# Fourier mixing by halves: a shorter DFT, head mixing folded into the weights, and the convolution's norm computed inside the attention

## The chip, the cores and the metric

The kernel runs on one core of a Trainium2 chip, in one launch, in float32 throughout. The metric is device time in microseconds of one execution; the median of several runs is compared. TensorE multiplies matrices (results land in PSUM banks of 512 float32 columns), ScalarE applies functions, VectorE does elementwise work and reductions, GpSimd small copies, and DMA queues issued from SyncE and ScalarE bring the weights from HBM.

## The reference, cut to what matters

Two networks run one after the other on 256 tokens of width 1024. The first has two layers; each projects the input (x, and in layer 0 also a context of 256 tokens, "two streams"), and mixes tokens in three branches: windowed attention, a convolution and a Fourier branch. The branches are gated by silu of projected gates and go through `w_out`. The parts that the change touches are these:

```
def conformer_conv(a, b_glu, conv_w, conv_b, ln_g, ln_b):
    u = a * jax.nn.sigmoid(b_glu)
    y = depthwise_conv(u, conv_w) + conv_b          # 31 taps, 256 channels
    return jax.nn.silu(layer_norm(y, ln_g, ln_b))

def fourier_mix(u, w_four, b_four):
    bn, n = u.shape[0], u.shape[1]
    uh = u.reshape(bn, n, FOUR_HEADS, FOUR_HEAD_DIM).astype(jnp.float32)
    f = jnp.fft.fftn(uh, axes=(1, 3), norm='ortho').real
    f = f.reshape(bn, n, FOUR_W).astype(u.dtype)
    return f @ w_four + b_four
```

The transform runs over 256 tokens and over the 64 channels of each of 4 heads. Its real part is the cosine transform over tokens mixed by the cosine matrix over channels, minus the sine transform over tokens mixed by the sine matrix over channels. The second network (a projection of 49 tiles, three attentions, gates, 16 experts) is not touched.

## The kernel before, in words

Every engine runs its own instruction list; the lists meet at semaphores. TensorE's order is written out by hand in `_(pe)`. Two PSUM banks `lin` and two `aux` are used in turn: `lin_bank` (L385) waits until the bank of two turns ago has been taken by ScalarE, `aux_bank` (L394) the same for VectorE. Weights stream from HBM in units of 1 MB into a ring of 6 slots (L861 to L874); SyncE loads a slot when TensorE has freed it. The last stage, the 16 experts, also loads units aside, into buffers that are free by then.

Layer 0 begins with the ada projection (L588, `ada_step`), then the norm, then the input tiles, `TILES1`, each a `product` of 8 accumulated matmuls of 512 columns (L607 to L610): the convolution's CB and CA tiles, the keys KK, the four query tiles QQ, a Fourier gate, and last the token-major tiles (values and Fourier input, L515) and the second Fourier gate (L525). In layer 1 most tiles have 256 columns. ScalarE copies each tile out of PSUM (L1057); for KK and QQ it also writes four quarters to RT (`half_turned`, L945), from which VectorE makes the rotary embedding (L1280). VectorE runs the convolution's 62 taps between the ropes (L1345 to L1366).

Between the last tile and the attention stands the stretch that the change rewrites (L611 to L645). TensorE computes the mean of the convolution over channels (L618), the DFT over tokens (L626; for each stream and each of 2 channel tiles a bank of 512 columns, 256 cosine and 256 sine), the variance (L631), the head mixing by the block matrices bc and bs (L637, L638), and the product with w_four (L643). VectorE subtracts the mean (L1370), squares (L1374), copies the DFT out to CS (L1378), takes the reciprocal of the norm (L1380), multiplies it in (L1382), copies the mixed result to FF (L1385) and adds b_four (L1388). ScalarE takes the square root (L1063) and applies the convolution's silu (L1067).

Attention (L538, L974, L1289) runs in pairs of items, 16 pairs in layer 0 and 8 in layer 1. For pair p TensorE computes scores (L551), transposes the probabilities of pair p-1 (L564) and multiplies pair p-2 by the values (L577). VectorE adds the mask and takes the maximum (L1313, L1316), ScalarE the exponential (L997), VectorE scales (L1297, L1301), ScalarE copies the transposes to PT (L987). Between these TensorE does "fills", matmuls of gate tiles (L456) and ada steps (L486). After attention ScalarE applies silu to the 8 gate tiles in the order `MIX_ORDER` (L1072), VectorE multiplies them in (L1397), and TensorE runs the output projection in the same order (L433 into aux).

Of the kernel before, what the change touches and what calls it, by code (L numbers as in the profile page):

```python
# [20 lines left out]
ALU = mybir.AluOpType  # L21
# [12 lines left out]
PAD = CONV_K // 2  # L34
N_EXP, EPG, TOPK = 16, 4, 64
# [30 lines left out]
MIX_ORDER = (4, 5, 6, 7, 0, 1, 2, 3)  # L66
# [38 lines left out]
for _name, _w in [("cos", 256), ("sin", 256), ("dft0", 512), ("dft1", 512), ("bc", 128), ("bs", 128),  # L105
                  ("band0", 512), ("band1", 512)]:
    C1[_name] = (_n, _n + _w)
    _n += _w
# [10 lines left out]
def constants():  # L119
# [24 lines left out]
    cs = np.concatenate([np.cos(ang), np.sin(ang)], 1)  # L144
# [20 lines left out]
def build(nc, w_stream, x_in, mem_in, cols_in, wfour_in, wsmall_in, c0_in, c1_in, c2_in, gf_in, rows, out):  # L165
    ctx = ExitStack()
    with ctx:
# [28 lines left out]
        wfour = sb("wfour", [P, DEPTH, 2, 256])  # L196
        wsmall = sb("wsmall", [P, KT, 24])
# [4 lines left out]
        warm = sb("warm", [P, 1])  # L202
# [15 lines left out]
        CS = G1[:, 0:2048].rearrange("p (f s n) -> p f s n", f=2, s=2)  # L218
        FF = G1[:, 2048:3072].rearrange("p (f s n) -> p f s n", f=2, s=2)
# [29 lines left out]
        for name, w in (("logits", 20), ("of_group", 16), ("place", 16), ("d", 5), ("e", 5), ("group", 4), ("sub", 4),  # L249
# [30 lines left out]
        roped, conv_done, conv_sq, conv_norm, conv_act = (  # L280
            sem(n) for n in ("roped", "conv_done", "conv_sq", "conv_norm", "conv_act"))
# [99 lines left out]
        def _(pe):  # L381
# [214 lines left out]
            for layer in range(DEPTH):  # L596
                L = f"l{layer}"
                ns = 2 if layer == 0 else 1
                for t in TILES1:
# [3 lines left out]
                    if t == GF + 1:  # L603
                        token_tiles((L, "tok"), [(H[:, s], tt, 384 if s < ns else P) for s in range(2) for tt in range(TT)],
                                    lambda: (lin_bank((L, GF + 1)), n, rhs))
                        continue
                    bank = lin_bank((L, t))  # L607
# [3 lines left out]
                if layer == 0:  # L611
                    pe.wait_ge(consts_in, 3 * 16)

                n = ns * SEQ
                pe.wait_ge(conv_done, layer + 1)
# [1159 lines left out]
```

## Time and profile before

| | |
|---|---|
| median of 3 runs | 1175.64 us (1171.31 to 1178.19) |
| profiled execution | 1173.04 us, span 1169.9 us |
| TensorE busy | 1074.7 us |
| VectorE busy | 406.0 us |
| ScalarE busy | 331.6 us |
| HBM traffic | 232.91 MB read |
| chain that ended last | PE 78%, DMA 12%, DVE 4%, ACT 3% |

In the profile PE is TensorE's matmuls and PEld its weight loads, DVE is VectorE, ACT ScalarE, SP SyncE. A float32 matmul stands in it as two records. The chain that ended last is followed back from the last instruction, at each step to what released it; a shorter step on it makes the program shorter as long as nothing else is then later. The granted clock is the share of 2.4 GHz that the chip allowed TensorE.

### The profile page before, as it was taken

Reading aid. Unit: us, or ns where it says so; the run is one execution under the profiler, and the core shown is the slowest. Engines: PE = TensorE matmul, PEld = TensorE weight load, DVE = VectorE, ACT = ScalarE, POOL = GpSimd, SP = SyncE. Lnnn points to the kernel's source line nnn. Section 1 sums busy time; section 2 is a strip of 40 time slices with the busy share of each in tenths; the row PEclk is TensorE's granted clock in tenths of the full one; section 3 lists DMA queues with packets and bytes.
Section 4 is the critical chain, followed back from the end, with each engine's and each line's share of the span. In section 5 each row is a group of like instructions: output and inputs, shape, how many; then the busy total and the mean of one; then the engine's idle time right before and its main releaser. Section 6 shows DMA issues by size and latency. Waiting matters only on the chain.

```text
span 1169.9 us, 13568 instructions
## 1 busy us (share of the span) xinstructions
PE 1074.7 (92%) x4952; PEld 676.1 (58%) x4952; DVE 406.0 (35%) x1182; ACT 331.6 (28%) x772; POOL 13.5 (1%) x60
## 2 busy tenths in 40 slices
PE   3899989999979998999999989879999998998885
PEld 0344434444457677768888456668888743443332
DVE  3269154432258444613932014641112400000004
ACT  2222133332043345234553024640011311111102
POOL 0000000000000000000000000000000000000010
PEclk9899999999989999999999999999999899999998
DMA  9897016452133222443433432036444589999995
GB/s 371 362 340 273 36 36 272 164 212 72 72 131 122 72 73 75 182 146 142 144 144 144 154 117 90 1 162 270 144 148 160 214 350 420 424 424 423 424 423 217
DMA packets 32903, 238.38 MB, mean 204 GB/s; under 512 B 3696, under 2 KB 3952, under 8 KB 6768
## 3 DMA queue, kind: packets, MB, share of 16 engines
q1 hardware_dynamic: 28768, 204.48, 44.9%
q10 hardware_dynamic: 3504, 31.06, 7.0%
q0 software_dynamic: 576, 2.10, 0.4%
q8 instruction: 35, 0.57, 0.2%
q14 instruction: 20, 0.16, 0.0%
HBM read 232.91 MB, written 19.40 MB: 216 GB/s over the span
## 4 chain that ended last, share of the span: by engine, by line
PE 78%; DMA 12%; DVE 4%; ACT 3%; issue 1%; SPq 1%; ACTq 0%; DVEq 0%
PE lin L433 28%; DMA ring<-w_stream 10%; PE aux L433 10%; PE lin L515 8%; PE sc L456 6%; PE lin L812 6%; PE aux L717 3%; PE aux L812 3%; DMA PT<-w_stream 3%; PE sc L551 2%; PE lin L564 2%; PE aux L577 2%; PE sc L771 2%; PE sc L486 1%; ACT S L997 1%
## 5 line engine op out<-in xcount | busy, mean ns | idle before, releaser
L433 PE MATMUL lin<-H,ring 128*128 128x256 f32 (+1 forms) x1360 | 341.9, 413 | 5.6 <-ACT H L1038 3.8
L433 PEld LDWEIGHTS lin<-H,ring 128*128 128x128 f32 x1360 | 261.5, 193 | 85.2 <-issue 51.3
L812 PE MATMUL lin<-ring,PR 128*64 128x512 f32 x400 | 94.5, 623 | 15.6 <-DMA ring<-w_stream 14.6
L515 PE MATMUL lin<-ring,H 128*128 128x512 f32 (+2 forms) x256 | 90.1, 513 | 0.0
L433 PE MATMUL aux<-Y,ring 128*128 128x512 f32 (+1 forms) x256 | 84.9, 493 | 3.1 <-DVE Y L1397 3.1
L812 PEld LDWEIGHTS lin<-ring,PR 128*64 128x64 f32 x400 | 32.2, 142 | 76.1 <-issue 76.1
L433 PEld LDWEIGHTS aux<-Y,ring 128*128 128x128 f32 x256 | 49.1, 192 | 38.2 <-issue 32.3
L515 PEld LDWEIGHTS lin<-ring,H 128*128 128x128 f32 x256 | 46.3, 190 | 42.7 <-issue 30.1
L456 PE MATMUL sc<-H,ring 128*128 128x512 f32 (+1 forms) x192 | 70.8, 503 | 0.0
L987 ACT ACTIVATE PT<-lin 128x512 f32<-128x512 f32 (+3 forms) x96 | 43.7, 467 | 93.3 <-PE lin L564 93.2
L1354 DVE SCALAR_TENSOR_TENSOR UN<-UN,cols 128x512 f32<-128x512 f32 (+1 forms) x120 | 64.5, 610 | 0.0
L953 ACT ACTIVATE RT<-lin 32x256 f32<-32x256 f32 x168 | 63.0, 375 | 2.6 <-DVE PR L1287 0.6
L997 ACT ACTIVATE S<-S,ST 128x513 f32<-128x513 f32 (+5 forms) x88 | 54.7, 621 | 10.6 <-DVE ST L1316 10.4
L564 PE MATMUL lin<-c,S 128*128 128x128 f32 x272 | 41.1, 285 | 13.7 <-DVE S L1301 10.1
L486 PE MATMUL sc<-ring,SC 128*32 128x512 f32 x192 | 28.5, 719 | 25.9 <-DMA ring<-w_stream 25.9
L564 PEld LDWEIGHTS lin<-c,S 128*128 128x128 f32 x272 | 31.5, 144 | 32.4 <-DVE S L1301 15.7
L456 PEld LDWEIGHTS sc<-H,ring 128*128 128x128 f32 x192 | 33.7, 189 | 27.4 <-issue 20.1
L1611 DVE TENSOR_TENSOR PR<-lin,PR 128x512 f32<-128x512 f32 x8 | 5.5, 691 | 122.7 <-PE lin L812 122.7
L717 PE MATMUL aux<-Y,ring 128*128 128x256 f32 x192 | 44.1, 390 | 3.0 <-DVE H L1478 2.5
L551 PE MATMUL sc<-PR 64*128 64x256 f32 (+3 forms) x240 | 43.3, 444 | 2.8 <-DVE ST L1313 2.1
L1297 DVE RECIPROCAL ST<-ST 128x1 f32<-128x1 f32 x88 | 14.4, 164 | 85.7 <-ACT S L997 85.0
L1284 DVE TENSOR_TENSOR RT<-RT,cb 128x256 f32<-128x256 f32 x42 | 17.8, 424 | 74.9 <-ACT RT L953 74.6
(236 smaller groups left out, 1068.8 us busy)
## 6 DMA issues: line engine op xcount, KB each, us to landing
ring<-w_stream SPq DMA_DIRECT2D x153, 1024.0 KB, 6.8
Y<-w_stream SPq DMA_DIRECT2D x14, 1024.0 KB, 15.6
UN<-w_stream SPq DMA_DIRECT2D x12, 1024.0 KB, 18.6
S<-w_stream SPq DMA_DIRECT2D x6, 1024.0 KB, 19.2
PT<-w_stream SPq DMA_DIRECT2D x6, 1024.0 KB, 20.9
rows<-PR ACTq DMA_DIRECT2D x7, 512.0 KB, 7.9
X<-x_in SPq DMA_DIRECT2D x2, 1024.0 KB, 8.4
UN<-w_stream ACTq DMA_DIRECT2D x2, 1024.0 KB, 6.4
```

The costliest lines, as they stand in the source:

```text
L433: m = mm(dst, w[:, k, :], rhs(k), start=n == 0, stop=n == KT - 1)
L456: m = mm(bank[:, 0:ns * SEQ], filling["w"][:, k, :], H[:, 0:ns, k, :], start=k == 0, stop=k == KT - 1)
L486: m = mm(bank[32 * j:32 * j + 32, :], SC[:, k0 + k, :], w[j // 2][:, 2 * k + j % 2, :], start=k0 + k == 0, stop=k0 + k == KT - 1)
L515: m = mm(bank[:, 0:width], src[:, k, tt * P:(tt + 1) * P], w[k // 4][:, k % 4, 0:width], start=k == 0, stop=k == KT - 1)
L551: m = mm(sc[:, x, a:b], it["qs"][n], it["ks"][n], start=True, stop=True, skip_group_check=True)
L564: m = tr(bank[:, j % 4 * P:(j % 4 + 1) * P], S[:, g % 4, 1 + j * P:1 + (j + 1) * P], t0("ident"))
L717: m = mm(bank[:, 0:SEQ], w[:, 4 * i + k, :], Y[:, 4 * b + k, :], start=k == 0, stop=k == 3)
L812: m = mm(bank[c, :], left[:, 4 * half + k, c], w[x][:, k, :], start=half + k == 0, stop=last)
L953: ins = fn(RT[32 * q:32 * q + 32, n % 2, :], bank[32 * r:32 * r + 32, 0:SEQ], ACT.Copy)
L987: fn(PT[:, g % 4, a:b], take()[:, 0:b - a], ACT.Copy).then_inc(lin_taken, 1)
L997: fn(e, e, ACT.Exp, bias=ST[:, g % 4, 1:2], scale=it["scale"], accum_out=ST[:, g % 4, 2:3]).then_inc(probs_ready, 1)
L1354: ins = v.scalar_tensor_tensor(out=CV[:, t, 0:ns, :], in0=u, scalar=w, in1=CV[:, t, 0:ns, :], op0=ALU.mult, op1=ALU.add)
```

## The change

The DFT matrices keep 256 of their 512 columns: the cosines of frequencies 0 to 128 and the sines of frequencies 1 to 127. The cosine half of the spectrum is even in the frequency and the sine half odd, so the other frequencies follow by adding and subtracting. The head mixing matrices bc and bs are multiplied into w_four once per layer, on TensorE, between the KK tile and the first QQ tile of layer 0; the results stay in WF. After the DFT, which now comes ahead of the mean and goes to the `lin` banks, ScalarE copies it to CS; the product with WF makes an even part (129 columns a stream) and an odd part (127 columns a stream) in one bank; VectorE writes even + b_four to frequencies 0 to 128, then even minus odd in reversed order to 129 to 255, then adds odd to 1 to 127. The mixing products, FF and its copies are gone. VectorE's reciprocal and norm of the convolution move into the attention, after the masks of pair 2. ScalarE's two silus of the convolution move behind the attention, ahead of gate 4; the gates' order becomes 6, 7, 4, 5, 0, 1, 2, 3. A load of the exponential's table is asked for ahead of attention. Each warm-up activation gets a column of its own.

```
-MIX_ORDER = (4, 5, 6, 7, 0, 1, 2, 3)
+MIX_ORDER = (6, 7, 4, 5, 0, 1, 2, 3)
...
-    cs = np.concatenate([np.cos(ang), np.sin(ang)], 1)
+    cs = np.concatenate([np.cos(ang)[:, :NYQ + 1], np.sin(ang)[:, 1:NYQ]], 1)
...
+        WF = sb("WF", [P, DEPTH, 2, 2, 256])
...
# TensorE
+                    if layer == 0 and t == QQ:
+                        pe.wait_ge(consts_in, 3 * 16)
+                        for l in range(DEPTH):
+                            for c, name in enumerate(("bc", "bs")):
+                                mm(lin_bank(("four", l, c))[:, :], t1(name), wfour[:, l, :, :], start=True, stop=True).then_inc(lin_ready, 1)
...
-                if layer == 0:
-                    pe.wait_ge(consts_in, 3 * 16)
...
+                pe.wait_ge(lin_taken, turn[L, "tok", 3] + 1)
+                for s in range(ns):
+                    bank = lin_bank((L, "dft", s))
+                    for f in range(2):
+                        for t in range(TT):
+                            m = mm(bank[:, f * 256:(f + 1) * 256], FT[:, s * TT + t, f * P:(f + 1) * P], t1(f"dft{t}"), start=t == 0, stop=t == 1)
+                    m.then_inc(lin_ready, 1)
                 pe.wait_ge(conv_done, layer + 1)
                 bank = aux_bank((L, "mean"))
...
-                pe.wait_ge(lin_taken, turn[L, "tok", 3] + 1)
-                for s in range(ns):
+                pe.wait_ge(lin_taken, turn[L, "dft", ns - 1] + 1)
+                for t in range(2):
+                    bank, c = aux_bank((L, "four", t)), slice(t * P, (t + 1) * P)
+                    even, odd = slice(0, ns * (NYQ + 1)), slice(ns * (NYQ + 1), ns * SEQ)
                     for f in range(2):
-                        bank = aux_bank((L, "dft", s, f))
-                        for t in range(TT):
-                            m = mm(bank[:, :], FT[:, s * TT + t, f * P:(f + 1) * P], t1(f"dft{t}"), start=t == 0, stop=t == 1)
-                        m.then_inc(aux_ready, 1)
+                        mm(bank[:, even], WF[:, layer, 0, f, c], CS[:, 0:ns, f, 0:NYQ + 1], start=f == 0, stop=f == 1)
+                    for f in range(2):
+                        m = mm(bank[:, odd], WF[:, layer, 1, f, c], CS[:, 0:ns, f, NYQ + 1:], start=f == 0, stop=f == 1)
+                    m.then_inc(aux_ready, 1)
...
-                for f in range(2):
-                    pe.wait_ge(aux_taken, turn[L, "dft", ns - 1, f] + 1)
-                    bank = aux_bank((L, "mix", f))
-                    mm(bank[:, 0:n], t1("bc"), CS[:, f, 0:ns, 0:256], start=True, stop=False)
-                    mm(bank[:, 0:n], t1("bs"), CS[:, f, 0:ns, 256:512], start=False, stop=True).then_inc(aux_ready, 1)
-                pe.wait_ge(aux_taken, turn[L, "mix", 1] + 1)
-                for t in range(2):
-                    bank = aux_bank((L, "four", t))
-                    for f in range(2):
-                        m = mm(bank[:, 0:n], wfour[:, layer, f, t * P:(t + 1) * P], FF[:, f, 0:ns, :], start=f == 0, stop=f == 1)
-                    m.then_inc(aux_ready, 1)
...
# ScalarE
+                    if layer == 0 and t == QQ:
+                        for l in range(DEPTH):
+                            for c in range(2):
+                                fn(WF[:, l, c, :, :].rearrange("p f n -> p (f n)"), take()[:, :], ACT.Copy).then_inc(lin_taken, 1)
...
+                for s in range(ns):
+                    fn(CS[:, s, :, :].rearrange("p f n -> p (f n)"), take()[:, :], ACT.Copy).then_inc(lin_taken, 1)
                 warm_up(ACT.Sqrt)
                 fn(RS[:, 0:n], take()[:, 0:n], ACT.Sqrt, bias=col("eps")).then_inc(lin_taken, 1)
-                act.wait_ge(conv_norm, layer + 1)
-                for t in range(2):
-                    v_ = CV[:, t, 0:ns, :]
-                    fn(v_, v_, ACT.Silu, bias=col(f"ln_b{layer}", t), scale=col(f"ln_g{layer}", t)).then_inc(conv_act, 1)
+                warm_up(ACT.Exp)
                 attention(L, lambda i: fill(layer, i))
                 act.wait_ge(fill_taken, 1 + len(FILLS[0]) + layer * len(FILLS[1]))
                 for k in MIX_ORDER:
+                    if k == 4:
+                        act.wait_ge(conv_norm, layer + 1)
+                        for t in range(2):
+                            v_ = CV[:, t, 0:ns, :]
+                            fn(v_, v_, ACT.Silu, bias=col(f"ln_b{layer}", t), scale=col(f"ln_g{layer}", t)).then_inc(conv_act, 1)
...
# VectorE
-                for s in range(ns):
-                    for f in range(2):
-                        v.tensor_copy(CS[:, f, s, :], take((L, "dft", s, f))[:, :]).then_inc(aux_taken, 1)
-                dve.wait_ge(lin_taken, turn[L, "var"] + 1)
-                after(step(v.reciprocal(RI[:, 0:n], RS[:, 0:n])))
                 for t in range(2):
-                    ins = v.tensor_tensor(CV[:, t, 0:ns, :], CV[:, t, 0:ns, :], RI[:, 0:n].rearrange("p (s n) -> p s n", s=ns), ALU.mult)
-                ins.then_inc(conv_norm, 1)
-                for f in range(2):
-                    v.tensor_copy(FF[:, f, 0:ns, :], take((L, "mix", f))[:, 0:n].rearrange("p (s n) -> p s n", s=ns)).then_inc(aux_taken, 1)
-                for t in range(2):
-                    bank = take((L, "four", t))
-                    v.tensor_scalar(YB[:, 6 + t, 0:ns, :], ...
+                    bank, y, b = take((L, "four", t)), YB[:, 6 + t, 0:ns, :], col(f"b_four{layer}", t)
...
+                    v.tensor_scalar(y[:, :, 0:NYQ + 1], even, b, None, ALU.add).then_inc(four_even, 1)
+                    dve.wait_ge(four_even, 2 * layer + t + 1)
+                    v.tensor_tensor(y[:, :, SEQ - 1:NYQ:-1], y[:, :, 1:NYQ], odd, ALU.subtract).then_inc(four_odd, 1)
+                    dve.wait_ge(four_odd, 2 * layer + t + 1)
+                    v.tensor_tensor(y[:, :, 1:NYQ], y[:, :, 1:NYQ], odd, ALU.add).then_inc(aux_taken, 1)
+
+                def conv_normed():
+                    dve.wait_ge(lin_taken, turn[L, "var"] + 1)
+                    after(step(v.reciprocal(RI[:, 0:n], RS[:, 0:n])))
+                    for t in range(2):
+                        ins = v.tensor_tensor(CV[:, t, 0:ns, :], CV[:, t, 0:ns, :], RI[:, 0:n].rearrange("p (s n) -> p s n", s=ns), ALU.mult)
+                    ins.then_inc(conv_norm, 1)
+
+                def between(p):
+                    if p == 2:
+                        conv_normed()
+                    if layer == 0 and 2 * p - 1 in ADA_TURNS:
+                        modulation(ADA_TURNS[2 * p - 1])
+
+                attention(L, between)
```

## Rows read from the trace of the kernel before

**Rows 1.** The page: busy time by engine, TensorE's.

```profile
PE 1074.7 (92%) x4952; PEld 676.1 (58%) x4952; DVE 406.0 (35%) x1182; ACT 331.6 (28%) x772; POOL 13.5 (1%) x60
```

**Rows 2.** Chain of waits, layer 0 ahead of attention: start us, us, what.

```profile
135.16 1.72 PE aux L618 x4
...
146.36 3.37 DVE RI L1380
...
157.69 1.06 PE sc L551 x4
```

**Rows 3.** Chain of waits, layer 1 ahead of attention.

```profile
384.84 3.46 PE lin L525 x16
...
397.26 1.99 PE aux L643 x8
399.26 1.06 PE sc L551 x4
```

**Rows 4.** Timeline ahead of attention: start us, us, engine, operation, [idle before <-releaser].

```profile
136.92 1.28 DVE L1370 TENSOR_TENSOR UN<-UN,aux 128x512 f32<-128x512 f32 x2 [20.53 <-PE aux L618]
...
152.29 5.40 PE L643 MATMUL aux<-PR,wfour 128*128 128x512 f32 x8 [3.26 <-DVE PR L1385]
...
155.18 0.75 DVE L1388 TENSOR_SCALAR Y<-aux,cols 128x512 f32<-128x512 f32 x1 [2.94 <-PE aux L643]
...
399.30 0.48 DVE L1388 TENSOR_SCALAR Y<-aux,cols 128x256 f32<-128x256 f32 x1 [0.38 <-PE aux L643]
```

**Rows 5.** ScalarE on the K tile (timeline); landing of w_four (DMA issues).

```profile
73.36 0.60 ACT L1057 ACTIVATE PR<-lin 128x512 f32<-128x512 f32 x1 [6.27 <-PE lin L433]
73.97 1.54 ACT L953 ACTIVATE RT<-lin 32x256 f32<-32x256 f32 x4
...
wfour<-wfour_in ACTq DMA_DIRECT2D x1, 512.0 KB, 14.5
```

**Rows 6.** Windows of 20 us: PE, PEld, DVE, ACT, POOL busy, PEclk, DMA share, GB/s.

```profile
80.00:100.00 20.00, 20.00 (x48) 8.93 (x47) 19.90 (x36) 6.30 (x15) 0.00 (x0) 1.00 1.04 365
...
140.00:160.00 20.00, 16.74 (x36) 6.72 (x36) 10.73 (x15) 5.01 (x6) 0.00 (x0) 0.91 0.00 1
...
260.00:280.00 20.00, 17.63 (x54) 8.05 (x53) 7.23 (x16) 8.81 (x15) 0.18 (x1) 0.91 0.15 53
...
320.00:340.00 20.00, 13.40 (x41) 8.80 (x40) 11.27 (x24) 11.34 (x21) 0.00 (x0) 0.74 0.28 100
...
380.00:400.00 20.00, 17.92 (x88) 13.30 (x87) 9.65 (x20) 7.11 (x12) 0.00 (x0) 1.00 0.15 53
```

**Rows 7.** Chain of waits, transposes of one item in layer 0's attention.

```profile
170.92 0.87 PE lin L564 x8
```

**Rows 8.** Timeline of layer 0's third pair: mask's last step, scaling, transposes.

```profile
170.90 0.15 DVE L1316 TENSOR_SCALAR ST<-ST 128x1 f32<-128x1 f32 x1
...
173.99 0.87 DVE L1301 TENSOR_SCALAR S<-S,ST 128x512 f32<-128x512 f32 x2
...
177.54 1.04 PE L564 MATMUL lin<-c,S 128*128 128x128 f32 x8
```

**Rows 9.** Timeline: the convolution's silus, then gates after attention in both layers.

```profile
151.07 1.52 ACT L1067 ACTIVATE UN<-UN,cols 128x512 f32<-128x512 f32 x2 [3.45 <-DVE UN L1382]
...
262.16 1.28 ACT L1072 ACT_TABLE_LOAD   x1
263.46 4.27 ACT L1072 ACTIVATE PR<-PR 128x512 f32<-128x512 f32 x8
...
265.01 7.51 PE L433 MATMUL aux<-Y,ring 128*128 128x512 f32 x13 [2.15 <-DVE Y L1397]
...
448.85 2.56 ACT L1072 ACTIVATE PR<-PR 128x256 f32<-128x256 f32 x8
```

**Rows 10.** Who the weight queue waited for; a window of the expert tail.

```profile
SPq L863 <- PE lin L433: 344.1, 43, 21.8
...
1020.00:1040.00 20.00, 20.00 (x112) 9.25 (x110) 2.03 (x6) 2.88 (x5) 0.00 (x0) 1.00 1.02 424
```

More of the change, by code:

```diff
@@ L34 @@
 PAD = CONV_K // 2
+NYQ = SEQ // 2
 N_EXP, EPG, TOPK = 16, 4, 64
@@ L104 @@
 _n = 0
-for _name, _w in [("cos", 256), ("sin", 256), ("dft0", 512), ("dft1", 512), ("bc", 128), ("bs", 128),
+for _name, _w in [("cos", 256), ("sin", 256), ("dft0", 256), ("dft1", 256), ("bc", 128), ("bs", 128),
                   ("band0", 512), ("band1", 512)]:
@@ L201, in build @@
         RO = sb("RO", [P, 192])
-        warm = sb("warm", [P, 1])
+        warm = sb("warm", [P, 16])
         CM = sb("CM", [P, TT, N_EXP])
@@ L217, in build @@
         G1 = P1[:, GA:GF, :, :].rearrange("p t s n -> p (t s n)")
-        CS = G1[:, 0:2048].rearrange("p (f s n) -> p f s n", f=2, s=2)
-        FF = G1[:, 2048:3072].rearrange("p (f s n) -> p f s n", f=2, s=2)
+        CS = G1[:, 0:1024].rearrange("p (s f n) -> p s f n", f=2, s=2)
         BVT = UN[:, 0:3072].rearrange("p (t n) -> p t n", t=TT)
@@ L279, in build @@
         dve_step = sem("dve_step")
-        roped, conv_done, conv_sq, conv_norm, conv_act = (
-            sem(n) for n in ("roped", "conv_done", "conv_sq", "conv_norm", "conv_act"))
+        roped, conv_done, conv_sq, conv_norm, conv_act, four_even, four_odd = (
+            sem(n) for n in ("roped", "conv_done", "conv_sq", "conv_norm", "conv_act", "four_even", "four_odd"))
         idx_mask, merged, gains_ready = sem("idx_mask"), sem("merged"), sem("gains_ready")
@@ L934, in _ @@
             fn = nc.scalar.activation
-            at = {"lin": 0, "sq": 0}
+            at = {"lin": 0, "sq": 0, "warm": 0}
             def take():
@@ L956, in warm_up @@
             def warm_up(f):
-                fn(warm[:, :], col("eps"), f)
+                n = at["warm"]
+                at["warm"] += 1
+                fn(warm[:, n:n + 1], col("eps"), f)
             def squares(name, src, ns, ready, between={}):
@@ L1383, in _ @@
-                ins.then_inc(conv_norm, 1)
-                for f in range(2):
-                    v.tensor_copy(FF[:, f, 0:ns, :], take((L, "mix", f))[:, 0:n].rearrange("p (s n) -> p s n", s=ns)).then_inc(aux_taken, 1)
-                for t in range(2):
-                    bank = take((L, "four", t))
-                    v.tensor_scalar(YB[:, 6 + t, 0:ns, :], bank[:, 0:n].rearrange("p (s n) -> p s n", s=ns),
-                                    col(f"b_four{layer}", t), None, ALU.add).then_inc(aux_taken, 1)
@@ L1390, in _ @@
-                attention(L, lambda p: modulation(ADA_TURNS[2 * p - 1]) if layer == 0 and 2 * p - 1 in ADA_TURNS else None)
+                for t in range(2):
+                    bank, y, b = take((L, "four", t)), YB[:, 6 + t, 0:ns, :], col(f"b_four{layer}", t)
+                    even = bank[:, 0:ns * (NYQ + 1)].rearrange("p (s n) -> p s n", s=ns)
+                    odd = bank[:, ns * (NYQ + 1):n].rearrange("p (s n) -> p s n", s=ns)
+                    v.tensor_scalar(y[:, :, 0:NYQ + 1], even, b, None, ALU.add).then_inc(four_even, 1)
[3 more added lines that the diff above has]
+                    v.tensor_tensor(y[:, :, 1:NYQ], y[:, :, 1:NYQ], odd, ALU.add).then_inc(aux_taken, 1)
```

## The prediction, made before the changed kernel was run

> **What bounds the kernel now.** I read the page first: TensorE is busy for 92% of the span [rows 1]. That only names the engine; what this change is worth depends on which wait ends last in the two places that it touches, the stretch between the last input tile and the first attention scores of layer 0 and of layer 1. So the chain of waits in order of time comes next. In layer 0 the last tile ends at 135.16 us, where the mean begins; the DFT and the variance follow on TensorE, then the chain leaves TensorE for the reciprocal of the convolution's norm on VectorE, and it comes back for the w_four products; the scores start at 157.69 [rows 2]. The stretch is 22.5 us long. In layer 1 the same chain is 10.96 us long (384.84 + 3.46 = 388.30 to 399.26) [rows 3]. Both chains have one engine at a time on them, so what is cut there is cut from the end.
>
> The price of a product is read from the same rows. A fp32 product stands as two records; two products of 512 columns took 1.72 us as four records, so 0.86 us for 512 columns and 0.43 for 256.
>
> **Layer 0, the stretch itself.** Removed: half of the DFT's columns (8 products of 512 become 8 of 256), the 4 head mixing products, the copies to FF, the wait for them. Kept: mean, variance. The w_four products keep their 2048 columns' worth: before 4 of 512; after, for each of two output tiles, 2 of 258 and 2 of 254, 2048 in all. The new order on TensorE is DFT 8 x 0.43 = 3.43, mean 1.72, w_four 3.43, variance 1.72: 10.3 us, if nothing waits. The waits, one by one. The mean needs the convolution, which VectorE had finished 20.53 us before it was asked for [rows 4]. The w_four products need two ScalarE copies of 128x512 (0.60 each, as the tile copy [rows 5]); the second DFT bank is complete 3.43 us in and copied 0.8 us later, under the mean's 1.72. The second w_four bank needs the mean taken, two subtractions, 1.28 together [rows 4], which end at about the moment the first w_four bank is full (cost 0 to 0.2; I take 0). The variance needs the squares, two more operations of that size, ready 0.6 us before. So 22.5 - 10.3 = **12.2 us less**. It splits into 4096 columns fewer (6.9), the 3.26 us in which TensorE waited for the FF copies, and about 2 us that the 8 records after that wait took too long: 5.40 us [rows 4] where 3.43 is the price. The granted clock has two levels, 2.4 and 1.2 GHz, so a mean of 0.91 over 20 us [rows 6] is 3.6 us at the lower one; in this stretch it comes right after the idle 3.26.
>
> VectorE must be free when the scores end, 1.06 us after they start. After the squares it has the six new operations on the halves, each of some 256 elements; the nearest row is the bias add that reads 256 from PSUM, 0.48 [rows 4]. Six of them plus waits are 3.0 us, from 8.0 to 11.0 us into the stretch, and the first scores are there at 11.4. The same six at 0.75, the price of 512 elements [rows 4], would be 1.6 us longer and 1.2 us late; no row has a reversed order of writing. I take 0 and keep 0 to 1.2. ScalarE loads the exponential's table after the square root; a load takes 1.28 us, and the next activation starts as it ends (262.16 and 263.46) [rows 9]. It is ready about 0.1 us after the first scores' bias, and TensorE asks for these probabilities only after 3 fills.
>
> **Layer 1.** Half the columns: DFT 4 x 0.43 = 1.72, mean 0.86, w_four as 8 products of 129 or 127 columns, variance 0.86. No product of 129 stands in the trace; four transposes of 128 columns took 0.87 as 8 records, 0.11 a record [rows 7]. 16 records are 1.75, where the 8 long ones took 1.99 [rows 3]. Sum 5.2, so 10.96 - 5.2 = **5.8 us less**. The columns give 3.4 of it, the rest is the wait for reciprocal and copies.
>
> **A rule against this change** concerns these short products. From 80 to 100 us TensorE's records of 512 columns fill all 20.00 us, one every 0.43, and 47 weight loads of 0.19 us (8.93 in all) stand beside them [rows 6]: loads hide behind columns, and the short records of rows 7 hide most of theirs too. The Trainium skill, page "TensorE: Matmul & The Clock Gate", section "Part 3: Packing small matmuls", says that a weight load overlaps running matmuls "only when row_grp differs", which is not so for these full 128-row weights. By that rule every record would pay its load of 0.19 us besides its columns; the change has the same 72 records in the two stretches and 8 more in the fold, so its sum would be 1.5 us smaller, 10.7, still within rival (a). The rows stand against it, and I don't follow it.
>
> **What the change adds: the fold.** Four products of 512 columns between the K tile and the first Q tile of layer 0: 3.43 us at the least. The two lin banks add a stall. After the K tile ScalarE spends 0.60 + 1.54 us on the copy and the quarter turns [rows 5], and the second fold product needs that bank. Step by step from the K tile's end: first product to 0.86; K's bank free at 2.4; second product to 3.3; third (needs the first bank's copy, done at 3.0) to 4.2; fourth to 5.0; Q's bank free at 5.0. So **5.0 us more**, 1.6 of it idle. Ends: 3.4 with full overlap, 6.9 with none. The constants are there: w_four landed 14.5 us after its issue [rows 5], which comes right after the last ada step at the start, and the fold comes at 73. VectorE is held 5 us in its ropes and finishes the convolution 5 us later, out of 20.5 us of slack. The ring gains 5 us.
>
> **The convolution's norm inside attention.** In layer 0 it puts 3.37 + 1.3 = 4.7 us [rows 2, 4] behind the masks of the third pair, in front of that pair's scaling. The masks' last step ended at 171.05; the norm would end at 175.7, the pair's scaling (0.87 after two short reciprocals) at 176.9, and TensorE's transposes of it start at 177.54 [rows 8]. The first scaled half is there by 176.5. It fits with about 0.6 to 1 us left, and the next pair's masks, 1.4 us late, are asked for 6.8 us later. In layer 1 it is 2.5 us at the same place. Cost 0; without the cover it would be 4.7 + 2.5.
>
> **The end of attention.** ScalarE now does two silus of the convolution between gates 7 and 4: 1.52 us in layer 0 [rows 9]. Gates come 0.53 us apart and TensorE eats one every 0.86. From 263.46: gates 6 and 7 to 264.5, the silus to 266.0, gate 4 to 266.6, VectorE 0.65, so TensorE could have it at 267.5; it reaches it at 265.01 + 1.72 = 266.7 at full clock, later with the lower clock that this place had (0.91 again) [rows 6]. **0.8 us more**, bounds 0 and 1.5. In layer 1 the first gate multiply is late for VectorE's last attention copy, not for ScalarE, whose gates began at 448.85, 1.9 us before the first multiply [rows 9]: cost 0, at most 1.1.
>
> **Sum.** 12.2 + 5.8 - 5.0 - 0.8 = 12.2 us. Against the profiled execution, 1173.04 us (span 1169.9), that is 1160.8. The median of the runs shown is 1175.64, 2.6 higher, which gives 1163.4. I take the middle, 1162.1. A measurement of this kernel can tell about 0.5% (5.9 us) from no change.
>
> Does the gain reach the end? In the expert tail DMA is full (424 GB/s) [rows 10] and TensorE waits for it. But over the span the weight queue waited 344.1 us for L433's products alone to free a ring slot [rows 10]: what the tail loads is let go by TensorE's progress, so it shifts with it.
>
> **Rivals.**
> (a) The forecast: 10 to 15 us less. The steps stand on rows of the same shapes. 75%.
> (b) Attention starts or runs late: the six half operations cost as 512 elements, the norm spills over its 0.6 us of cover, or the fold's 1.6 us idle brings the clock down once more. After 2.15 us of idle before 265.01 [rows 9] it did fall, for 3.6 us of the window of 260 to 280, which costs 1.8; in layer 1, where TensorE idled 2.1 us in two pieces between 380 and 400, it stayed at 1.00 [rows 6]. Together 4 to 7 us of the gain: about 1167. 14%.
> (c) The gain is swallowed by the weight stream: 12 us less for TensorE, the tail no earlier, 1170 to 1175. For it speaks the full DMA of the tail; against it the queue's own waits [rows 10]. 7%.
> (d) Slower: after the fold's idle the clock stays at its lower level. Place: the Q tiles. Each tile of 6.87 us then costs another 6.87; it decides from 24 us at the low level. Four Q tiles would cost 27.5: 1173.04 - 12.2 + 27.5 = 1188. The longest low stretch (0.74 from 320 to 340, so 10.4 us) stood with 6.6 us of idle in it [rows 6]; here full products follow at once. 4%.
>
> **Numbers.** Faster by over 0.5%: (a) and most of (b), 0.86; within 0.5%: (c) and the rest, 0.10; slower 0.04. The range: largest gain 15.5 (fold at 3.4, no gate stall, one clock drop fewer) from the level of 1171.3 to 1173 gives 1156; smallest gain worth keeping 5.6 (fold at 6.9, one more drop of 1.8, gates 1.5 and 1.1, VectorE 1.2 late) from 1175.6 gives 1170.
>
> **What would show it.** Right: last tile to first scores 10.3 us in layer 0 and 5.2 in layer 1, no idle before the w_four products; 5 us between K and Q tiles; transposes of the third pair unmoved in the period of 6.8. Wrong: the first masks late for VectorE (rival b), a lower granted clock after the fold (b, d), longer ring waits at the ada fills or in the tail by as much as was gained (c).

## The result

The changed kernel took 1156.97 us (median of 4 runs, 1152.65 to 1161.35) against 1174.24 us (1171.31 to 1178.19) for the kernel before; the ratio is 0.9871 with a 95% interval of 0.9823 to 0.9919. It is faster, by 9.5 to 21 us; the forecast of 1162.1 us lies 5 us above the median, and the median lies 1 us inside the lower end of the forecast's range (1156 to 1170). The experiments below run the same kernel again beside 17 runs of the kernel before: 0.9886 (0.9855 to 0.9917).

The page of the changed kernel's profiled execution (1156.09 us) shows what a page can show of this, and no more: a span 15.6 us shorter at the same share of TensorE [rows 1].

```profile
span 1154.3 us, 13587 instructions
...
PE 1060.9 (92%) x4960; PEld 673.4 (58%) x4960; DVE 401.7 (35%) x1180; ACT 333.2 (29%) x779; POOL 13.7 (1%) x60
```

The chain of waits in order of time shows the places (start us, us, what). First the fold, between the key tile and the first query tile:

```profile
36.98 37.16 PE lin L434 x80
...
74.16 0.60 ACT PR L1064
...
76.35 2.94 PE lin L612 x6
79.29 34.34 PE lin L434 x80
```

The fifth tile ends at 74.14 and the sixth starts at 79.29: 5.15 us, part of it on ScalarE's copy and turns. Then layer 1 ahead of attention, where [rows 3] had 10.96 us with VectorE and ScalarE on the chain:

```profile
378.94 1.73 PE lin L624 x8
380.66 0.86 PE aux L629 x4
381.52 0.54 PE aux L637 x4
382.06 0.45 PE aux L639 x4
382.51 0.58 PE aux L637 x4
383.08 0.45 PE aux L639 x4
383.53 0.87 PE lin L644 x4
384.39 1.06 PE sc L552 x4
```

The chain stays on TensorE for 5.45 us. In layer 0 the timeline shows the same, with VectorE beside it (columns as in [rows 4]):

```profile
140.97 3.62 PE L624 MATMUL lin<-cb,UN 128*128 128x256 f32 x16
...
148.87 0.48 DVE L1391 TENSOR_SCALAR Y<-aux,cols 128x258 f32<-128x258 f32 x1
149.38 0.42 DVE L1393 TENSOR_TENSOR Y<-Y,aux 128x254 f32<-128x254 f32 x1
...
151.14 0.42 DVE L1395 TENSOR_TENSOR Y<-Y,aux 128x254 f32<-128x254 f32 x1
151.40 1.13 PE L552 MATMUL sc<-PR 64*128 64x512 f32 x4
...
152.56 0.75 DVE L1324 CUSTOM_DVE_ANT_0 S<-sc,cb,SK 128x512 f32<-128x512 f32 x1 [1.00 <-PE sc L552]
```

From the last tile's end at 141.13 to the scores at 151.47 on the chain it is 10.3 us, where [rows 2] had 22.5. VectorE is done with the halves at 151.56 and waits 1.00 us for the scores; the reversed write (L1393) costs what the straight one does (L1395).

**Where 15.6 us came from**, from equal landmarks in the two profiles (starts of the same operations on TensorE, for the gate multiply on VectorE; of a layer's last tile, the start of its last record):

```
stretch                                    before    after    gained
start to the last tile of layer 0           134.6    140.5     -5.9
to layer 0's first scores                    23.0     10.9     12.1
to its last scores                           98.1     95.9      2.2
to its first gate multiply                    8.5      8.5      0
to the last tile of layer 1                 123.7    122.8      0.9
to layer 1's first scores                    11.3      5.7      5.6
to its first gate multiply                   51.5     51.5      0
to the memory's mean square                  11.0     12.4     -1.4
to the second network's first scores        225.8    227.5     -1.7
to its first branch product                  90.0     87.5      2.5
to the end                                  392.4    391.1      1.3
```

The rows at 12.1 and 5.6 and most of the -5.9 are the steps of the prediction. In the -1.4 stands a wait of 1.10 us that this profile of the kernel before does not have. The rest, some 4 us net, lies in stretches where TensorE does the same in both kernels.

### The profile page after: what moved, and what is told of

Its sections match the earlier page's. It is cut to its first block, busy times and chain, and to the rows that moved or that the text cites. A ratio compares the mean times of both kernels' runs of the same rounds, so it can differ in the third digit from the quotient of the medians.

```text
span 1154.3 us, 13587 instructions
## 1 busy us (share of the span) xinstructions
PE 1060.9 (92%) x4960; PEld 673.4 (58%) x4960; DVE 401.7 (35%) x1180; ACT 333.2 (29%) x779; POOL 13.7 (1%) x60
## 4 chain that ended last, share of the span: by engine, by line
PE 78%; DMA 12%; ACT 4%; DVE 3%; issue 1%; SPq 1%; ACTq 0%; DVEq 0%
PE lin L434 30%; DMA ring<-w_stream 10%; PE aux L434 9%; PE lin L516 8%; PE sc L457 6%; PE lin L813 6%; PE aux L718 3%; PE aux L813 3%; DMA PT<-w_stream 3%; PE sc L552 2%; PE lin L565 2%; PE sc L772 2%; PE aux L578 2%; PE sc L487 1%; ACT S L1000 1%
## 5 line engine op out<-in xcount | busy, mean ns | idle before, releaser
L813 PE MATMUL lin<-ring,PR 128*64 128x512 f32 x400 | 92.8, 613 | 17.4 <-DMA ring<-w_stream 16.4
L565 PE MATMUL lin<-c,S 128*128 128x128 f32 x272 | 40.3, 281 | 14.1 <-DVE S L1312 10.4
L578 PE MATMUL aux<-PT,UN 128*64 128x128 f32 (+1 forms) x544 | 41.7, 286 | 0.2 <-ACT PT L990 0.2
## 6 DMA issues: line engine op xcount, KB each, us to landing
Y<-w_stream SPq DMA_DIRECT2D x14, 1024.0 KB, 15.6
```

What stands on the lines that cost most here:

```text
L565: m = tr(bank[:, j % 4 * P:(j % 4 + 1) * P], S[:, g % 4, 1 + j * P:1 + (j + 1) * P], t0("ident"))
L578: m = mm(bank[pair[x]["bank"]], pair[x]["vs"][j], PT[:, (g + x) % 4, j * P:(j + 1) * P], start=j == 0, stop=j == nk - 1)
L813: m = mm(bank[c, :], left[:, 4 * half + k, c], w[x][:, k, :], start=half + k == 0, stop=last)
```

## The experiments

Each kernel was timed in 5 rounds beside the kernel before, in three sets on three chips: the first four below; then the fold one tile earlier, the DFT twice, norm and silus moved, and the better fold; last the idle filled and the split fold only. A ratio is always to the 17 runs of the kernel before in the same set. "The changed kernel" stands for its repeated run of the first set (median 1159.27 us, ratio 0.9886), so a difference of medians across sets also holds a difference between chips. Two theories stood against each other. **S**: the steps add up, and what is over is TensorE's clock. **T**: something in the change also helps what follows.

**The changed kernel again.** No edit.

> The changed kernel, unaltered. Theory S (the steps add up): by the two profiles the parts that the change rewrites are worth 11 us (fold +5.2, layer 0 stretch -12.2, layer 1 stretch -5.5, end of layer 1 +1.3), and the other 4 to 5 us of the first comparison are drops of TensorE's clock that fell in one profile and not in the other, in code that is the same in both. Then this is 11 to 13 us below the kernel before, and in its profile the untouched stretch from the end of the last tile ahead of the second network's attention to its first branch product is between the two lengths seen, not reliably the shorter one. Theory T (something in the change helps the second network too): 16 to 18 us below, and the untouched stretch is the shorter one again.

Measured: 1159.27 us, ratio 0.9886 (0.9855 to 0.9917), 13.4 us below before. In its profile the stretch from the second network's first scores to its last took 83.8 us, where the first profile of the same kernel had 80.6 and the kernel before 83.4. In the nine other profiles it took 83.4 to 85.0. So the short stretch does not belong to the change, and T falls by the profiles; by the time alone it would not, as the interval of the gain (9.7 to 17.0 us) reaches into its 16 to 18. S had the stretch to the first branch product between the two lengths seen, 90.0 and 87.5 us; it took 90.7. The windows (columns as in [rows 6]) show what the 3 us are; first this run, then the first profile of the changed kernel:

```profile
720.00:740.00 20.00, 16.29 (x162) 12.45 (x158) 12.48 (x44) 11.78 (x29) 0.00 (x0) 0.91 0.00 1
740.00:760.00 20.00, 16.57 (x140) 12.91 (x141) 12.66 (x53) 10.90 (x32) 0.00 (x0) 0.91 0.00 1
```

```profile
720.00:740.00 20.00, 15.70 (x166) 12.35 (x167) 14.32 (x51) 12.60 (x31) 0.00 (x0) 1.00 0.00 1
740.00:760.00 20.00, 16.64 (x151) 12.88 (x149) 12.97 (x59) 12.45 (x38) 0.00 (x0) 1.00 0.01 2
```

Nearly the same instructions (this run enters the stretch 1.4 us later), TensorE idle for 3.4 to 4.3 us in each window: in one execution the granted clock was lower in both windows, in the other it stayed at 1.00.

**The fold alone.** The kernel before, with WF added:

```
+                    if layer == 0 and t == QQ:
+                        pe.wait_ge(consts_in, 3 * 16)
+                        for l in range(DEPTH):
+                            for c, name in enumerate(("bc", "bs")):
+                                mm(lin_bank(("four", l, c))[:, :], t1(name), wfour[:, l, :, :], ...)
...
+                                fn(WF[:, l, c, :, :]..., take()[:, :], ACT.Copy).then_inc(lin_taken, 1)
```

> The kernel before with the change's fold added (four products of 512 columns and their four copies between the key tile and the first query tile of layer 0); its result is used by nothing. Theory S: 5.1 us slower than before (3.4 of products, 1.6 to 1.8 of idle for the key tile's bank), all of it on the end. Rival: the fold hides under a later wait for the ring, because the ring gains 5 us there: 0 to 2 us slower, and the ring waits of layer 0's ada fills are shorter. Rival: the idle brings the clock down: 7 us.

Measured: 1173.65 us, ratio 1.0022 (0.9995 to 1.0049), so 2.6 us slower, between 0.6 faster and 5.7 slower. That does not tell 5.1 from 0 to 2; the profile has to. Its chain shows the fold at the price expected: tiles end at 73.57 and go on at 78.72.

```profile
37.29 36.28 PE lin L434 x80
...
75.78 2.94 PE lin L612 x6
78.72 1.29 PE lin L434 x3
```

The ring's waits did not shrink in return (4.0 us of them in layer 0, 4.3 before). What shrank is the time at the low clock: 57 us a run on average (12 runs), against 62.6 in 51 runs of the kernel before. The section on the clock below takes that up.

**Norm ahead of attention again.** The changed kernel, with

```
+                conv_normed()
+
                 def between(p):
-                    if p == 2:
-                        conv_normed()
```

> The changed kernel with the convolution's reciprocal and norm on VectorE put back ahead of attention (right after the Fourier halves); the silus stay behind attention. The first masks are then 4.3 us late in layer 0 and 2.5 in layer 1. Theory S: TensorE asks for the first pair's probabilities only 7.5 us after its scores, so only what goes beyond that cover counts: 1 to 2 us slower than the changed kernel in layer 0, under 1 in layer 1, together 1 to 2.5 (about 10 below before). Rival: the whole delay counts, 6.8 us slower than the changed kernel.

Measured: 1160.4 us, ratio 0.9897 (0.9863 to 0.9931), 1.1 us above the run of the changed kernel beside it. The timeline of layer 0:

```profile
152.16 3.35 DVE L1399 RECIPROCAL RI<-RS 128x512 f32<-128x512 f32 x1 [0.67 <-ACT RS L1072]
...
156.75 0.74 DVE L1324 CUSTOM_DVE_ANT_0 S<-sc,cb,SK 128x512 f32<-128x512 f32 x1
...
158.41 2.08 PE L552 MATMUL sc<-PR 64*128 64x512 f32 x4 [2.32 <-DVE ST L1324]
```

The window over that wait (columns as in [rows 6]):

```profile
156.00:164.00 8.00, 5.68 (x18) 2.67 (x18) 5.32 (x18) 2.19 (x6) 0.37 (x2) 0.79 0.23 95
```

The masks came 4.2 us late and TensorE waited 2.32 us, though not where I expected: the second pair's scores need the first pair's banks, and they are asked for earlier than the probabilities. Behind the wait the records are slow, four of scores in 2.08 us instead of 1.13, with a granted clock of 0.79 over the window where the changed kernel has 1.00. From the first scores to the first transposes it is 11.5 us against 7.6: of the 4.2 us in layer 0 the profile shows 3.9 as paid, 2.3 as idle and 1.6 as slow clock. In layer 1 it shows 0.1 of 2.5 (first to last scores 41.3 us against 41.2). Together 4.0 us, more than S had and less than the rival's 6.8; the medians differ by 1.1 only, with intervals that overlap.

**Norm and silus ahead of attention.** Besides the edit above:

```
+                act.wait_ge(conv_norm, layer + 1)
+                for t in range(2):
...
+                    fn(v_, v_, ACT.Silu, ...).then_inc(conv_act, 1)
                 warm_up(ACT.Exp)
                 attention(L, lambda i: fill(layer, i))
```

> The changed kernel with norm and silus both ahead of attention (gates' order as in the change). ScalarE then loads silu's table, does two silus, loads the exponential's again after the norm, so the first exponential is 6 us later in layer 0 and about 4 in layer 1; the end of layer 1 gets its 1.1 us of wait for VectorE's sums back. Theory S: 3 to 4.5 us slower than the changed kernel in layer 0, 1 to 2 in layer 1, less 1.3 at the end of layer 1: 3 to 5 us slower in all. Rival (the move as such is worth little): within 1.5 us of the changed kernel.

Measured: 1162.41 us, ratio 0.9912 (0.9882 to 0.9943), 3.1 above the changed kernel and 2.0 above the kernel with the norm alone ahead; from layer 1's last scores to the memory's mean square it has 21.3 us, as before, where the changed kernel had 22.7 and 23.0. The direction and size are those of S, with intervals that overlap. The places are not quite: in layer 0 the first transposes come 11.5 us after the first scores, no later than with the norm alone ahead, in layer 1 first to last scores take 0.3 us more than in the changed kernel instead of 1 to 2, and at the end of layer 1 TensorE still waits 0.97 us for VectorE's sums.

**The fold one tile earlier.** `t == QQ` becomes `t == KK` on both engines.

> The changed kernel with the fold one tile earlier, ahead of the key tile: the tile before it has no quarter turns, so its bank is free 1.5 us sooner. Theory S: the idle inside the fold goes, 1.4 to 1.6 us faster than the changed kernel, and its profile shows 3.5 us for the eight records of the fold instead of 5.1. Rival: ScalarE's quarter turns then hold up the next tile instead, no difference.

Measured: 1157.88 us, ratio 0.9858 (0.9822 to 0.9893). The chain:

```profile
35.59 29.40 PE lin L434 x64
64.98 3.62 PE lin L612 x8
```

3.62 us instead of 5.15: 1.5 us of the fold were a wait for the key tile's bank. The median is 1.4 us below the changed kernel's, but by the ratios, each to its own set, it would be 3.3, so the times alone would not tell it. Of the rival, that the next tile is held up instead, the chain shows nothing: the tiles go on at 68.61.

**The DFT twice.** The changed kernel with `for f in (0, 1, 0, 1)` in the DFT.

> The changed kernel with every DFT product done twice (same values into the same bank): 8 more products of 256 columns in layer 0, 4 in layer 1, as many columns as the halves took away. Theory S: columns count in full, 3.4 + 1.7 = 5.1 us slower than the changed kernel. Rival (the stretch was bound by its waits, not by columns): under 2 us slower.

Measured: 1161.59 us, ratio 0.9887 (0.9848 to 0.9926). By landmarks the stretch of layer 0 is 14.4 us instead of 10.9, that of layer 1 7.5 instead of 5.7: +5.3 us, columns in full, as S says. The time does not show it: the median is only 2.3 us above the changed kernel's, and the ratios are the same (0.9887 and 0.9886), which alone would speak for the rival. There was less time at the low clock again (46.8 us a run against 53.7).

**Norm and silus moved, nothing else.** The kernel before with `conv_normed` at `p == 2`, the silus ahead of gate 4, the new gate order and the early table.

> The kernel before with one part of the change alone: reciprocal and norm of the convolution after the masks of the third pair, its silus behind attention, the gates' order, the exponential's table asked for early. No halves, no fold. Theory S: the reciprocal and norm leave the chain between variance and w_four product. VectorE can copy the mixed result at once: in layer 0 the wait of 3.26 us shrinks to about 1.3 and the slow clock behind it (2 us) mostly goes, in layer 1 some 2 us go; less 1.3 at the end of layer 1. Sum 3 to 5 us faster than before. Rival: nothing, because the copies of the DFT and the mixing still alternate between TensorE and VectorE: within 1 us.

Measured: 1168.34 us, ratio 0.9957 (0.9930 to 0.9983), 5.0 us faster than before. Layer 0 ahead of attention (timeline), to be set beside the w_four line of [rows 4] with its 3.26 of idle and 5.40 of work:

```profile
147.76 0.69 DVE L1384 COPY PR<-aux 128x512 f32<-128x512 f32 x1 [1.03 <-PE aux L638]
148.50 3.70 PE L643 MATMUL aux<-PR,wfour 128*128 128x512 f32 x8 [0.78 <-DVE PR L1384]
```

The stretch shrank from 23.0 to 18.8 us in layer 0 and from 11.3 to 9.7 in layer 1. So of the 12.1 and 5.6, the moved norm gives 4.2 and 1.6 where the mixing is kept; the halves and the fold give the rest, 7.9 and 4.0, of which the columns that are gone are 6.9 and 3.4 at the price of a product. At the end of layer 1 this kernel too has TensorE wait for VectorE, 1.35 us.

**The idle filled.** The kernel before, with three products nobody reads, ahead of layer 0's w_four products:

```
+                if layer == 0:
+                    for _ in range(3):
+                        mm(sc[:, 0, 0:512], t1("bc"), wfour[:, 0, :, :], start=True, stop=True)
                 pe.wait_ge(aux_taken, turn[L, "mix", 1] + 1)
```

> The kernel before with three products of 512 columns, used by nothing, in the 3.26 us for which TensorE idles ahead of layer 0's w_four products (2.6 us of them, so nothing is held up). Theory S says that 2 us of the gain in layer 0 were the slow clock behind that idle: the eight records take 3.5 us instead of 5.4, the granted clock stays at 1.00 there, and the kernel is about 2 us faster than before although it does more. Rival (those records are slow for another reason, their weights or their banks): still 5.4 us.

Measured: 1168.72 us, ratio 0.9959 (0.9930 to 0.9988): faster by 4.8 us (1.4 to 8.2) with more work.

```profile
149.25 2.74 PE L641 MATMUL sc<-wfour,cb 128*128 128x512 f32 x6
...
152.67 3.70 PE L646 MATMUL aux<-PR,wfour 128*128 128x512 f32 x8 [0.68 <-DVE PR L1388]
```

The eight records took 3.70 us instead of 5.40, at a granted clock of 1.00 instead of 0.68 (window of just these records). Their slowness was the clock. In both profiles that have the idle of 3.26 us there (before; before with the fold) the clock falls behind it, in the two in which it is filled or gone (this one; norm and silus moved) it does not.

**A better fold, and VectorE's order.** The changed kernel with the fold of layer 0 (2 products) ahead of the key tile, that of layer 1 behind layer 0's output projection, and in layer 1:

```
                 if layer == 1:
-                    add_squares(range(KT), 1)
+                    add_squares(range(5), 1)
                 for t in range(KT):
                     bank = take((L, "out", t))
...
                     ins.then_inc(aux_taken, 1)
+                    if layer == 1 and t == 0:
+                        add_squares(range(5, KT), 1)
                     add_squares([t - 1], ns)
```

> The changed kernel, improved at the two places that the profiles point to. The fold of layer 0 stands ahead of the key tile (2 products), the fold of layer 1 behind layer 0's output projection, where TensorE idles for the squares; and in layer 1 VectorE takes the first output tile before the last three sums of squares of the memory, so that TensorE need not wait 1.1 us for its bank. Theory S: the fold costs 1.7 instead of 5.2 us and the wait at the end of layer 1 goes: 4.5 us faster than the changed kernel. Rival: the second fold delays layer 1's mean square or norm by as much as it saves ahead: 2.5 to 3 us faster only.

Measured: 1154.61 us (1150.52 to 1157.13), ratio 0.9830 (0.9795 to 0.9866), 4.7 us below the repeated run of the changed kernel, and by the ratios 6.6. Its timeline, at the two folds and at the end of layer 1:

```profile
66.93 1.98 PE L511 MATMUL lin<-wfour,cb 128*128 128x512 f32 x4
...
68.75 11.75 PE L434 MATMUL lin<-H,ring 128*128 128x512 f32 x27
...
312.06 1.88 PE L511 MATMUL lin<-wfour,cb 128*128 128x512 f32 x4
...
314.68 1.10 PE L473 MATMUL lin<-SA,c 128*128 128x512 f32 x2 [0.74 <-DVE SA L1254]
...
435.21 10.60 PE L434 MATMUL aux<-Y,ring 128*128 128x256 f32 x48 [0.95 <-DVE Y L1423]
```

The first fold costs 1.8 us, the second none: TensorE is idle for VectorE's sum after it. The output projection runs through its first three tiles (16 records each) in 10.60 us without a wait.

**The split fold only.** The same without VectorE's new order.

> The changed kernel with the fold split as in the eighth kernel, VectorE's order at the end of layer 1 as in the change. Theory S: 3.4 us faster than the changed kernel, and in layer 1 the output projection still waits 1.1 us for its bank, so from the first gate multiply to the memory's mean square it takes 12.4 to 12.7 us again, where the eighth kernel had 11.0. Rival (the eighth kernel's short stretch came from the clock): 11.0 here too.

The eighth kernel is the one just above. Measured: 1156.3 us, ratio 0.9851 (0.9803 to 0.9899), 3.0 us below the changed kernel by the medians and 4.1 by the ratios. The wait is back, at 0.62 us, and from gate multiply to mean square it takes 11.9 us, short of the 12.4 I had expected and above the 11.0 of the kernel with the new order. These two profiles are a clean pair, since attention's last value products took 3.61 and 3.62 us in them. The new order is worth 0.9 us.

```profile
440.80 3.72 PE L434 MATMUL aux<-Y,ring 128*128 128x256 f32 x16 [0.62 <-DVE X L1429]
```

**The clock over all runs.** Every run lists its mean granted clock. As it has two levels, the time at the low one is (1 - mean) / 0.5 of the span. Half of it is what the clock would cost if TensorE were the bound all the time, so it is an upper estimate.

```
kernel                       runs   mean us   low us   mean us less half of low
before                         51    1173.3     62.6    1142.0
before, with the fold          12    1174.7     57.3    1146.1
before, norm moved             12    1168.3     57.0    1139.8
before, idle filled            12    1168.9     54.5    1141.6
changed                        10    1158.5     53.7    1131.7
changed, norm ahead             6    1160.8     56.0    1132.8
changed, norm and silus ahead   6    1162.4     57.6    1133.6
changed, fold a tile earlier    6    1157.8     51.2    1132.2
changed, DFT twice              6    1161.5     46.8    1138.1
changed, fold split, sums       6    1154.6     57.2    1126.0
changed, fold split only        6    1155.2     52.3    1129.0
```

The pooled gain of the change is 14.8 us (12.7 to 16.9); less the clock it is 10.3 (9.0 to 11.7). Corrected in this way the fold costs 4.1 and the doubled DFT 6.4, around the 5.1 and 5.3 that the profiles show. The fold one tile earlier shows no gain so (0.4 us slower, give or take 2.2) where its profile shows 1.5: steps of that size are below what the times can tell. Kernels that differ only ahead of attention differ by up to 8 us in low time, and it falls in other places: from profile to profile 0 to 6.8 us of it in layer 0's attention, 0 to 10.2 in the second network's. Which place is hit changes with an unchanged program too, as the first experiment shows. What decides it was not settled.

## Why the prediction was right

**Layer 0's stretch.** Forecast 10.3 us, measured 10.3 on the chain. The split also held: 4096 columns (the doubled DFT gives half of them back at 3.5 us), the wait of 3.26, and about 2 us of slow clock, which the filled idle shows as 5.40 to 3.70. VectorE's six operations were forecast at 3.0 us and took 2.7, with 1.00 us left instead of 0.4. The first part of rival (b) needed them at 0.75 each; at 0.42 to 0.48 it falls, and its other two parts, the norm's cover and a drop behind the fold, fall below.

**Layer 1's stretch.** Forecast 5.2, measured 5.45. The short products came to 2.0 us instead of 1.75, 0.11 to 0.145 a record. The Trainium skill's rule on weight loads (page "TensorE: Matmul & The Clock Gate", section "Part 3: Packing small matmuls") would have had each of them pay 0.19 us more; with 4 records in 0.45 us they pay none. The trace speaks against the rule for these float32 loads. The same section also lets a load run ahead when it goes to the background weight buffer; whether these do, no run here shows.

**The fold.** Forecast 5.0, measured 5.15, and the part that I called idle was removed by moving it one tile: 3.62.

**The norm inside attention.** Forecast 0, measured 0. The reciprocal stood at 164.75, the scaling behind it ended at 170.41, and TensorE began the transposes at 171.32, one period of 6.78 after the pair before.

```profile
164.54 1.04 PE L565 MATMUL lin<-c,S 128*128 128x128 f32 x8
...
164.75 3.34 DVE L1399 RECIPROCAL RI<-RS 128x512 f32<-128x512 f32 x1
...
169.53 0.88 DVE L1312 TENSOR_SCALAR S<-S,ST 128x512 f32<-128x512 f32 x2
...
171.32 1.04 PE L565 MATMUL lin<-c,S 128*128 128x128 f32 x8
```

I had counted the move's whole worth as the wait that it ends. Put back in the new order it costs 4.0 us in the profile, 1.6 of it clock; taken alone in the old order it gives 5.8 on the stretches, 1.7 of it clock. Its worth depends on what else stands on the chain.

**The gates of layer 0.** Forecast 0.8, bounds 0 and 1.5. The profile of the change shows 0: the projection takes 56.88 us on the chain in both kernels, and in both the clock is low under its first tile. Where a profile had no such drop, it shows 0.6 to 0.7: from the first gate multiply to the mean square 59.0 to 59.1 us in the kernels with the silus behind attention (norm ahead; norm moved; DFT twice), 58.4 in the kernel before with the fold. With the drop it is 60.1 to 60.3 us whether the silus stand behind attention or ahead of it.

**The step that failed** is the end of layer 1: "cost 0, at most 1.1". It cost 0.9 to 1.0 us. The silus did not delay the gates, as I had worked out, but they delay what ScalarE does next, the squares for the memory's norm. VectorE sums these ahead of taking the first output tile (`add_squares(range(KT), 1)`), and TensorE waits for that bank. I had asked who waits for the gates, and not who is queued behind the silus on ScalarE. The timeline of the changed kernel, then the same two ends in the kernel before:

```profile
433.15 1.28 ACT L1083 ACT_TABLE_LOAD   x1
...
435.08 1.08 ACT L1081 ACTIVATE UN<-UN,cols 128x256 f32<-128x256 f32 x2
...
441.64 2.00 ACT L971 ACTIVATE SQ<-X 128x256 f32<-128x256 f32 x4 [0.24 <-DVE SA L1248]
444.11 0.87 DVE L1423 SCALAR_TENSOR_TENSOR X<-aux,MOD,X 128x256 f32<-128x256 f32 x2
444.64 3.72 PE L434 MATMUL aux<-Y,ring 128*128 128x256 f32 x16 [1.10 <-DVE X L1423]
...
448.20 0.59 PE L473 MATMUL lin<-SA,c 128*128 128x256 f32 x2
```

```profile
447.56 1.28 ACT L1072 ACT_TABLE_LOAD   x1
...
461.73 0.59 PE L472 MATMUL lin<-SA,c 128*128 128x256 f32 x2
```

From that table load to the memory's mean square it is 15.0 us in all seven profiles with the silus behind attention and VectorE's old order, 14.1 to 14.2 in the four with them ahead, and 14.2 in the kernel with the new order. The difference is what the two silus take on ScalarE (1.08 us here). The idle of 1.10 us is not the price by itself: two profiles with the silus ahead (norm and silus ahead; idle filled) have 0.97 and 0.99 us of it too. There the value products at attention's end ran in 1.97 us; in the other two (before; before with the fold) they took 3.6, so TensorE came to the projection later and found the bank free. The 1.4 to 1.7 us between gate multiply and mean square hold some of that clock as well.

**The sum.** With what the profiles show (12.2 and 5.5 gained; 5.15 for the fold, 0 to 0.7 for the gates, 0.9 to 1.0 for the end of layer 1) the steps give about 11 us, where the forecast was 12.2. Two us of layer 0's 12.2 were a clock drop, so the part without the clock is about 9 to 9.6; the runs, corrected for the clock, show 10.3. The first comparison showed 17.3, more than the 10 to 15 of rival (a), because its runs of the changed kernel also had less low clock elsewhere; all runs pooled show 14.8. That term I had only as "one drop more or less" of 1.8 us; it is the size that was off, by up to two such drops. So the steps were right but for that one, and that the first median fell inside the range, by 1 us, is in part luck: one drop fewer still, and it would have been below it. The range itself was added up wrong: a fold at 3.4 (1.6), no gate stall (0.8) and one drop fewer (1.8) make the largest gain 16.4 us, not 15.5.

**Rivals.** (c), the gain swallowed by the weight stream, falls: the tail from the first expert product to its last took 226.5 us before and 226.6 after, simply earlier. (d), the clock low for long after the fold's idle: in the window of 60 to 80 us, which holds the 1.37 us of idle, it is 1.00. I had also read the 2.1 us of idle in layer 1 before the change as two pieces; it is one of 2.08 us ahead of the w_four products, with no drop behind it.

```profile
60.00:80.00 20.00, 18.63 (x44) 7.74 (x43) 10.48 (x18) 5.68 (x11) 0.00 (x0) 1.00 1.02 361
```

## What to carry to other kernels

Cost a moved operation on both sides of its engine: who waits for its result, and what stands behind it in the queue, there and on the engines that this feeds. Compare two profiles by stretches between equal landmarks before reading a gain into their difference; a stretch of unchanged code that differs is the noise, and here it was over a quarter of the gain. Start such a stretch on the engine that sets its length: at the end of layer 1 that is ScalarE, and from its table load on the profiles of one order agree to 0.1 us. A constant product that is made once costs nothing where TensorE already idles for another engine: look for that place before putting it between two tiles whose banks are slow to come free.

## What was not expected

Adding work made the kernel faster. Three products that nobody reads, put where TensorE idled for 3.26 us, gained 4.8 us (1.4 to 8.2), of which the stretch itself shows 1.7; the mean low time fell by 8 us, more than the one drop that was removed. Why the others went as well is open.

Idle of about 1.4 us (the fold) brought no drop in any of six profiles; 2.15 to 2.17 us at the end of layer 0's attention did in eight profiles (before and the changed kernel among them) and not in four (before with the fold among them), with the same work around it.

A table load on ScalarE starts as the activation ahead of it ends (151.51 + 0.69, then 152.21) and is followed at once by the next one (152.21 + 1.28, then 153.51). The Trainium skill, page "ScalarE: Activation LUTs", section "What ACT_TABLE_LOAD costs", adds about 1380 ns of drain to the load at every switch to another set; the rows here show none of it.

```profile
151.51 0.69 ACT L1072 ACTIVATE RS<-lin,cols 128x512 f32<-128x512 f32 x1 [4.78 <-PE lin L644]
152.21 1.28 ACT L961 ACT_TABLE_LOAD   x1
...
153.51 0.20 ACT L961 ACTIVATE warm<-cols 128x1 f32<-128x1 f32 x1
```
